# Sparse attention heads of a two-block layer: masks and gates prepared once, fewer VectorE operations per head, exponentials in one piece

## The reference, cut to what matters

```python
s_c = einsum(qb, kc) * scale + head_bias(dist_c)
p_c = masked_softmax(s_c, dist_c >= 0)          # exp masked again, sum kept above 1e-30
p_s = masked_softmax(s_s, dist_s >= 0)
p_w = masked_softmax(s_w, mask_w)
o = g0 * (p_c @ vc) + g1 * (p_s @ vs) + g2 * (p_w @ vw)   # gates g: one per position, head and branch
```

## Time and profile before

| | us |
|---|---|
| median of 3 runs (4032.55 to 4039.31) | 4033.61 |
| the profiled execution | 4030.8 |
| its span, first instruction to last | 4028.9 |
| busy in the span: PE / DVE / ACT / POOL | 3857.7 / 1769.7 / 600.3 / 1241.4 |

### The profile page before, as it was taken

How to read it: one execution, slowest core, us unless ns; L and a number is a source line. 1 busy time by engine, 2 the same in 40 slices (tenths; PEclk the granted TensorE clock), 3 DMA queues, 4 the chain that set the end, 5 groups by cost and what they waited for, 6 DMA issues and landing times.

```text
span 4028.9 us, 65270 instructions
## 1 busy us (share of the span) xinstructions
PE 3857.7 (96%) x28244; PEld 3561.4 (88%) x28244; DVE 1769.7 (44%) x3203; ACT 600.3 (15%) x1315; POOL 1241.4 (31%) x783
## 2 busy tenths in 40 slices
PE   8999999999999999999999999997798899999997
PEld 7888888888788998999999998776597899999997
DVE  1344425540313513111144455723422688887544
ACT  0333311111111011000000000222302211111001
POOL 0000000003222774777740000001150477775000
PEclk9999999999999999999999999998899999999999
DMA  6566654456654443444444554354142344444442
GB/s 239 195 225 225 220 207 170 160 191 215 194 179 159 155 168 110 170 170 171 170 158 160 172 206 170 140 128 158 45 160 97 115 168 168 168 168 163 167 158 79
DMA packets 109118, 668.81 MB, mean 166 GB/s; under 512 B 23056, under 2 KB 27472, under 8 KB 78496
## 3 DMA queue, kind: packets, MB, share of 16 engines
q1 hardware_dynamic: 64208, 549.01, 37.6%
q0 software_dynamic: 21088, 69.73, 5.8%
q10 hardware_dynamic: 23536, 45.92, 3.2%
HBM read 611.34 MB, written 53.25 MB: 165 GB/s over the span
## 4 chain that ended last, share of the span: by engine, by line
PE 89%; DVE 4%; issue 3%; ACT 2%; POOL 1%; POOLq 1%; DVEq 1%; ACTq 1%; DMA 0%
PE product_bank L550 46%; PE product_bank L598 31%; PE product_bank L392 3%; PE mixer_bank L742 1%; PE mixer_bank L758 1%; POOL arena L519 1%; POOLq L521 1%; POOLq L518 0%; POOL arena L522 0%; ACT xT L859 0%; PE mixer_bank L1271 0%; PE mixer_bank L1285 0%; PE mixer_bank L1122 0%; ACTq L2276 0%; DVE arena L1357 0%
## 5 line engine op out<-in xcount | busy, mean ns | idle before, releaser
L598 PE MATMUL product_bank<-hT,weight_ring 128*128 128x256 f32 x3648 | 812.4, 381 | 0.0
L598 PEld LDWEIGHTS product_bank<-hT,weight_ring 128*128 128x128 f32 x3648 | 689.5, 190 | 103.2 <-issue 10.2
L550 PE MATMUL product_bank<-hT,weight_ring 128*128 128x128 f32 x3680 | 457.6, 277 | 14.1 <-DVEq L1628 5.8
L550 PEld LDWEIGHTS product_bank<-hT,weight_ring 128*128 128x128 f32 x3680 | 435.8, 193 | 16.7 <-issue 6.8
L550 PE MATMUL product_bank<-arena,weight_ring 128*128 128x128 f32 x3200 | 398.5, 275 | 0.0
L550 PEld LDWEIGHTS product_bank<-arena,weight_ring 128*128 128x128 f32 x3200 | 378.5, 192 | 0.6
L517 POOL TENSOR_TENSOR arena<-weight_ring 128x1024 f32<-128x1024 f32 x89 | 212.8, 2391 | 479.5 <-PE product_bank L550 307.7
L574 DVE TENSOR_TENSOR arena<-product_bank,arena 128x128 f32<-128x128 f32 x127 | 36.9, 290 | 730.9 <-PE product_bank L550 730.9
L2601 DVE SCALAR_TENSOR_TENSOR arena<-arena 128x256 f32<-128x256 f32 x176 | 322.4, 1870 | 14.2 <-ACT arena L2566 10.9
L520 POOL TENSOR_TENSOR weight_ring<-weight_ring 128x1024 f32<-128x1024 f32 x111 | 272.1, 2452 | 0.0
L550 PE MATMUL product_bank<-hT,arena 128*128 128x128 f32 x2048 | 250.9, 277 | 0.2 <-DVE hT L506 0.2
(11 more groups left out here) (495 smaller groups left out, 5353.3 us busy)
## 6 DMA issues: line engine op xcount, KB each, us to landing
weight_ring<-in_weights SPq DMA_DIRECT2D x213, 2048.0 KB, 8.0
weight_ring<-in_weights SPq DMA_DIRECT2D x128, 512.0 KB, 5.6
weight_ring<-in_weights SPq DMA_DIRECT2D x64, 384.0 KB, 5.8
units<-out_stage ACTq DMA_DIRECT2D x87, 256.0 KB, 7.8
rwkv_keep<-arena ACTq DMA_DIRECT2D x16, 1282.0 KB, 6.1
arena<-rwkv_keep POOLq DMA_DIRECT2D x8, 1280.0 KB, 7.3
arena<-units POOLq DMA_DIRECT2D x36, 256.0 KB, 3.4
arena<-units POOLq DMA_DIRECT2D x48, 128.0 KB, 6.0
```

The lines of the kernel that those rows point to most:

```text
L550: mm = pe.matmul(bank[:, at * P:at * P + P], lhs[:, j, :], rhs[:, j, :], start=g == 0 and n in (0, 3) and j == 0, stop=g == n_groups - 1 a ...
L598: mm = pe.matmul(psg[b][:, half * T:half * T + T], lhs, rhs, start=k == 0, stop=k == 15)
```

## The change

In the sparse heads only, nothing on PE, POOL or SP is edited. Before the loop DVE scales the compressed bias by 8, adds the mask to it for all heads at once, and lays out the gates of all heads in one array, with the rows that see no compressed block set to zero. In the loop the compressed scores are one operation (L2325 goes), the four maxima are two over pairs, the two negations are one, the mask on the exponentials (L2340) and the floor (L2344) go, the two gate products are one, and the two scalings of the compressed part are one. On ACT all exponentials of head h+1 stand together, ahead of the wait for head h's output and of its copy.

```diff
-        n_H, n_kc, n_vc, n_pos = carve(120, 64, 256, 2, at=at + 2 * sum(NSA_BUFS))
+        n_H, n_kc, n_vc, n_pos, n_gate = carve(120, 64, 256, 2, 96, at=at + 2 * sum(NSA_BUFS))
...
+        ngate = n_gate.rearrange("p (h w q) -> p h w q", w=3, q=2)
...
-            def exponentials(h, w):
+            def exponentials(h):
                 n_s, n_pt, n_cs, n_ct, n_st = nsa_bufs[h % 2]
                 act.wait_ge(sem("attn_max"), NSA_SOFT_AT + h + 1)
-                for qb, (a, z) in enumerate([(256, 384), (0, 256)]):
-                    n = 2 * w + qb
-                    s = n_s[:, 384 * w + a:384 * w + z]
-                    act.activation(s, s, ACT.Exp, scale=HSCALE, bias=n_st[:, 8 + n:9 + n],
-                                   accum_out=n_st[:, 16 + n:17 + n])
-                if w == 0:
-                    return
+                for w in range(2):
+                    for qb, (a, z) in enumerate([(256, 384), (0, 256)]):
+                        n = 2 * w + qb
+                        s = n_s[:, 384 * w + a:384 * w + z]
+                        act.activation(s, s, ACT.Exp, scale=HSCALE, bias=n_st[:, 8 + n:9 + n],
+                                       accum_out=n_st[:, 16 + n:17 + n])
                 for qb in range(2):
                     s = n_cs[:, 16 * qb:16 * qb + 15]
-                    act.activation(s, s, ACT.Exp, bias=n_st[:, 12 + qb:13 + qb])
+                    act.activation(s, s, ACT.Exp, scale=HSCALE, bias=n_st[:, 12 + qb:13 + qb])
                 act.drain().then_inc(sem("attn_exp"), 1)
 
-            exponentials(0, 0)
-            exponentials(0, 1)
+            exponentials(0)
             for h in range(NH):
...
                 act.drain().then_inc(sem("attn_pt"), 1)
                 if h + 1 < NH:
-                    exponentials(h + 1, 0)
+                    exponentials(h + 1)
                 act.wait_ge(sem("attn_out"), NSA_AT_HEAD + h + 1)
                 act.activation(hT[r, 8 + b, :], bank[0][r, 0:256], ACT.Copy).then_inc(sem("attn_head_done"), 1)
-                if h + 1 < NH:
-                    exponentials(h + 1, 1)
                 if h in (5, 11):
                     store_unit(act, *LATE[3 + h // 6])
...
-            dve.tensor_copy(nBC, pm[1][:, 0:480].rearrange("p (q n h) -> p q h n", q=2, h=NH))
+            dve.tensor_scalar(nBC, pm[1][:, 0:480].rearrange("p (q n h) -> p q h n", q=2, h=NH), 1 / HSCALE, None, ALU.mult)
             dve.drain().then_inc(sem("bias_rows_ready"), 1)
             dve.wait_ge(sem("bias_rows_stored"), 16)
             dve.wait_ge(sem("nsa_gates"), 1)
...
+            dve.tensor_tensor(nBC, nBC, cadd.unsqueeze(2).to_broadcast([P, 2, NH, NCMP]), ALU.add)
+            by_head = ng.rearrange("p q (h w) -> p h w q", w=3)
+            dve.tensor_copy(ngate[:, :, 0:2, :], by_head[:, :, 1:3, :])
+            dve.tensor_tensor(ngate[:, :, 2, :], by_head[:, :, 0, :], cmul[:, :, 0].unsqueeze(1).to_broadcast([P, NH, 2]),
+                              ALU.mult)
+            dve.drain()
             for h in range(NH):
...
-                dve.scalar_tensor_tensor(cs, bank[0][:, 384:416].rearrange("p (q n) -> p q n", q=2)[:, :, 0:15], HSCALE,
-                                         nBC[:, :, h, :], ALU.mult, ALU.add)
-                dve.drain()
-                dve.tensor_tensor(cs, cs, cadd, ALU.add)
+                dve.tensor_tensor(cs, bank[0][:, 384:416].rearrange("p (q n) -> p q n", q=2)[:, :, 0:NCMP], nBC[:, :, h, :],
+                                  ALU.add)
                 dve.wait_ge(sem(f"nsa_bias{h % 2}"), 32 * (h // 2 + 1))
...
-                for w in range(2):
-                    dve.reduce_max(n_st[:, 2 * w:2 * w + 1], n_s[:, 384 * w + 256:384 * w + 384], AX.X)
-                    dve.reduce_max(n_st[:, 2 * w + 1:2 * w + 2], n_s[:, 384 * w:384 * w + 256], AX.X)
-                dve.drain()
+                dve.reduce_max(n_st[:, 0:4:2], both[:, :, 256:384], AX.X)
+                dve.reduce_max(n_st[:, 1:4:2], both[:, :, 0:256], AX.X)
                 dve.reduce_max(n_st[:, 4:6], cs, AX.X)
                 dve.drain()
-                dve.tensor_scalar(n_st[:, 8:12], n_st[:, 0:4], -HSCALE, None, ALU.mult)
-                dve.tensor_scalar(n_st[:, 12:14], n_st[:, 4:6], -1.0, None, ALU.mult).then_inc(sem("attn_max"), 1)
+                dve.tensor_scalar(n_st[:, 8:14], n_st[:, 0:6], -HSCALE, None, ALU.mult).then_inc(sem("attn_max"), 1)
                 dve.wait_ge(sem("attn_exp"), NSA_SOFT_AT + h + 1)
-                dve.tensor_tensor(cs, cs, cmul, ALU.mult)
-                dve.drain()
                 dve.reduce_sum(n_st[:, 20:22], cs, AX.X)
                 dve.drain()
-                dve.tensor_scalar(n_st[:, 16:22], n_st[:, 16:22], 1e-30, None, ALU.max)
-                dve.drain()
                 dve.reciprocal(n_st[:, 16:22], n_st[:, 16:22])
                 dve.drain()
-
-                f = n_st[:, 24:30].rearrange("p (w q) -> p q w", w=3)
-                s = n_st[:, 16:22].rearrange("p (w q) -> p q w", w=3)
-                dve.tensor_tensor(f[:, :, 0:2], s[:, :, 0:2], ng[:, :, 3 * h + 1:3 * h + 3], ALU.mult)
-                dve.tensor_tensor(f[:, :, 2:3], s[:, :, 2:3], ng[:, :, 3 * h:3 * h + 1], ALU.mult)
+                dve.tensor_tensor(n_st[:, 24:30], n_st[:, 16:22], n_gate[:, 6 * h:6 * h + 6], ALU.mult)
                 dve.drain()
                 for w in range(2):
...
-                for qb in range(2):
-                    v = n_cs[:, 16 * qb:16 * qb + 15]
-                    last = dve.tensor_scalar(v, v, n_st[:, 28 + qb:29 + qb], None, ALU.mult)
-                last.then_inc(sem("attn_probs"), 1)
+                dve.tensor_tensor(cs, cs, n_st[:, 28:30].unsqueeze(2).to_broadcast([P, 2, NCMP]), ALU.mult)\
+                    .then_inc(sem("attn_probs"), 1)
```

More of the change, by code:

```diff
@@ L2319, in nsa_dve @@
                 bank = nsa_banks(h)
-                cs = n_cs.rearrange("p (q n) -> p q n", q=2)[:, :, 0:15]
+                cs = n_cs.rearrange("p (q n) -> p q n", q=2)[:, :, 0:NCMP]
+                both = n_s.rearrange("p (w n) -> p w n", w=2)
                 dve.wait_ge(sem("attn_scores"), NSA_AT_HEAD + h + 1)
-                dve.scalar_tensor_tensor(cs, bank[0][:, 384:416].rearrange("p (q n) -> p q n", q=2)[:, :, 0:15], HSCALE,
-                                         nBC[:, :, h, :], ALU.mult, ALU.add)
-                dve.drain()
-                dve.tensor_tensor(cs, cs, cadd, ALU.add)
+                dve.tensor_tensor(cs, bank[0][:, 384:416].rearrange("p (q n) -> p q n", q=2)[:, :, 0:NCMP], nBC[:, :, h, :],
+                                  ALU.add)
                 dve.wait_ge(sem(f"nsa_bias{h % 2}"), 32 * (h // 2 + 1))
                 for w in range(2):
-                    dve.tensor_tensor(n_s[:, 384 * w:384 * w + 384], bank[w][:, 0:384], nbias[:, h % 2, :], ALU.add)\
+                    dve.tensor_tensor(both[:, w, :], bank[w][:, 0:384], nbias[:, h % 2, :], ALU.add)\
                         .then_inc(sem("nsa_biased"), 1)
                 dve.drain()
-                for w in range(2):
-                    dve.reduce_max(n_st[:, 2 * w:2 * w + 1], n_s[:, 384 * w + 256:384 * w + 384], AX.X)
-                    dve.reduce_max(n_st[:, 2 * w + 1:2 * w + 2], n_s[:, 384 * w:384 * w + 256], AX.X)
-                dve.drain()
+                dve.reduce_max(n_st[:, 0:4:2], both[:, :, 256:384], AX.X)
+                dve.reduce_max(n_st[:, 1:4:2], both[:, :, 0:256], AX.X)
                 dve.reduce_max(n_st[:, 4:6], cs, AX.X)
                 dve.drain()
-                dve.tensor_scalar(n_st[:, 8:12], n_st[:, 0:4], -HSCALE, None, ALU.mult)
-                dve.tensor_scalar(n_st[:, 12:14], n_st[:, 4:6], -1.0, None, ALU.mult).then_inc(sem("attn_max"), 1)
+                dve.tensor_scalar(n_st[:, 8:14], n_st[:, 0:6], -HSCALE, None, ALU.mult).then_inc(sem("attn_max"), 1)
                 dve.wait_ge(sem("attn_exp"), NSA_SOFT_AT + h + 1)
-                dve.tensor_tensor(cs, cs, cmul, ALU.mult)
-                dve.drain()
                 dve.reduce_sum(n_st[:, 20:22], cs, AX.X)
-                dve.drain()
-                dve.tensor_scalar(n_st[:, 16:22], n_st[:, 16:22], 1e-30, None, ALU.max)
                 dve.drain()
```

## The result

The changed kernel takes 4004.69 us in the median of 4 runs (4000.66 to 4007.26), the kernel before 4033.08 beside it: a ratio of 0.9924, 95% interval 0.9908 to 0.9939, so 28 us less. 4004.0 was predicted. The profiled execution of the changed kernel took 4000.66 us, the lowest of its four, with a span of 3998.9, 30.0 less than the span of before.

The account below looks back on a forecast made before the run. No engine is full; a loop of waits between PE, ACT and DVE bounds the sparse heads. 10.0 + 17.0 + 3.0 + 0.2 = 30 off the profiled 4030.8 gives 4001, plus 2.8 for the median: 4004 us, range 3995 to 4015.

Parts of the forecast that it names:

- Even steps: Eight even steps of the sparse heads: from 90.2 to 73.2 us, PE binding, mostly at 2.4 GHz; 17.0 us gained.
- The rival with the low clock: PE stays at 1.2 GHz at the start of even steps, 1.6 us more in each of four: 4011; chance 0.14.
- Plain odd steps: Steps 3, 5, 9, 11, 13 of the sparse heads: 9.4 becomes 7.4 us each; 10.0 us gained.
- PE binds: In the new odd step PE's side, 7.3 to 7.4 us, narrowly outlasts DVE's 7.1.
- The POOL steps: Steps 1 and 7, where POOL sums weights: 12.5 to 15.0 and 10.7 to 13.2 us; 3.0 us gained, from 0.5 to 5.6.
- the middle I took: Steps 1 and 7: gain of 3.0 us, taken between scalings before L522 and scalings waiting for its end.
- the strict reading: Steps 1 and 7: each scaling can be caught by a POOL instruction; the total ends 2.5 us later, at 4006.
- Head 0: Before and in head 0: 1.1 us of operations added, front and back give back 1.3; 0.2 us gained.
- Removed operations only: Rival: ACT and PE hinder each other, leaving 1.25 us in each of 16 steps, 20 in all: 4014; chance 0.09.
- Given back in `out2`: Rival: out2's weights arrive no earlier than now, so PE waits there: 4033; chance 0.03.
- Slower: Rival: grouped maxima with strided results run far below one element per cycle: 4045; chance 0.04.
- X = 6.5: X is the time from scores to maxima, 2.65 expected; at 6.5 each of 7 step pairs loses 1.6 us: 4045.

Follow-up runs that it names:

- e2_dve_only: The changed kernel with the ACT order of before (exponentials in two pieces, the second behind head h's output): 4015.25 us.
- e1_act_only: The kernel before with the ACT edit alone (exponentials in one piece): 4014.99 us.
- e3_back_undone: The changed kernel with the mask on the compressed exponentials and the floor 1e-30 put back into each head: 4008.14 us.
- e4_front_undone: The changed kernel with four maxima and two negations per head again, ahead of the exponentials: 4008.71 us.
- e7_memory_behind: The changed kernel with one memory product whole in step 0 and the other two behind the last head: 4058.69 us.
- the halves: The kernel before with the ACT edit alone, and the changed kernel with the ACT order of before: 18.7 and 18.4 us under the kernel before.
- e6_sums_spread: The changed kernel with each of POOL's two sums of weights cut into three parts, one ahead of the loads of each odd head 5 to 15: 3986.82 us.
- e8_sums_gaps: The changed kernel with POOL's eight sum instructions sent one at a time, each after VectorE gives a head's maxima: 3996.03 us.

## Why the prediction was right, point by point

- **Even steps, 17.0 forecast.** They gave 17.1: the eight took 90.1 before and take 73.0. PE became the bound, and at 2.4 GHz: 8.55, where 8.7 was taken. The closeness of the sum is partly luck: step 0 took 11.04 where 10.4 was taken, 0.6 too little, and the four plain steps and step 14 (6.94 for 7.2) together 0.9 too much. That the clock stays up after a wait under 1 us, a choice in the prediction, held here and, for waits of 1.42, in `e2_dve_only`. The rival with the low clock, at 4011, did not come in this kernel; it did in single steps of `e1_act_only`, `e3_back_undone` and `e4_front_undone`. The prediction says that every even step of the kernel before starts at 1.2 GHz; steps 4 and 6 start at 2.4 (first transpose 0.33 us) and the clock falls just behind, for a grant of 0.85 and 0.84 over the step, so the reading holds for their lengths.
- **Plain odd steps, 10.0 forecast.** 10.35. The order of events was right to 0.1: maxima at 2.67 (2.65 forecast), exponentials 2.31, copy at 5.06 (5.0). The back is 1.87 where 2.04 was taken, which costs nothing here, as it has slack. "PE binds" was right in that the scores release the turn, but loosely put: PE's own work is 6.75 of 7.40. What binds is the chain through the copy, as `e4_front_undone` and `e7_memory_behind` show.
- **The POOL steps, 3.0 forecast, from 0.5 to 5.6.** 2.1, between the middle I took and the 0.5 of the strict reading. The path was that of the strict reading, which ends behind L522, but with 0.3 from L522's end to the turn where 1.3 was taken: step 1 is 1.3, 12.5 of the sum and 0.3, 14.1 in all. The Trainium skill (SBUF — State Buffer, SBUF: two separate sides) has the engine that starts first hold the shared ports for the whole instruction and lets reductions pass; the rows agree: the maximum L2336 takes its 0.68 beside L517, the negation L2339 ends as L517 ends, the gates L2345 get in 0.05 before L519 starts, and three of the four scalings stand behind one POOL instruction each.
- **Head 0, 0.2 forecast.** From VectorE's start to the turn it was 8.22 us (2749.45 to 2757.67) and is 7.78, 0.4 less: the added work takes 0.95 (2749.96 to 2750.91) where 1.1 was taken. But that execution reached the stage 0.5 later (row below), so turn 0 lies at 2757.74.

The added work of head 0, in VectorE's timeline after (L2318 and L2319 follow it, 0.19 and 0.20), against the earlier trace rows:

```profile
2749.96 0.66 DVE L2316 TENSOR_TENSOR arena<-arena,consts 128x480 f32<-128x480 f32 x1 [54.31 <-ACT arena L2262]
```

- **Removed operations only, 4014.** Excluded: the halves are not additive, and 0.53 us put back cost 0.1 per odd step and nothing in even ones.
- **Given back in `out2`, 4033.** The rest of the span is 1099.5 where it was 1100.1.
- **Slower, 4045.** The maxima over pairs take 0.42 and 0.68 with strided results; to be slower than before, by the prediction's estimate the front would have had to last 3 us longer than it does.

The sum was 30; 29.4 came in this stage (179.4 to 150.0), 0.6 in the rest of the span. The parts miss by +0.1, +0.35, -0.9 and +0.2, so that the total is closer than its POOL term. Against the runs' median the gain is 28.4: the profiled execution lay 4.0 under the median after and 2.3 before. Small slips in the prediction change none of this: the upper bound of the POOL steps is 5.5 by its own figures (28.7 less 23.2), its own range 4001 to 4008 and not 4000 to 4009, the loss at X = 6.5 is 1.5 per pair and not 1.6.

## What to carry to other kernels

Write the loop between engines as a sum of stretches and put each engine's own work beside it as a floor: the gain of an edit is its share up to that floor, and two edits that reach the same floor do not add. After such a change look for what is late next; here it was another engine's work in one piece, whose cost depended on where it lay, and cutting it up gave 18 us more for a few lines. Order the copies of one engine so that no wait for a slow neighbour stands ahead of work that is already due.

## What the runs showed of the hardware

- TensorE's clock fell to 1.2 GHz in single steps after short waits of PE: 0.65 us (`e3_back_undone`, step 6), 0.65 and 0.39 (the same, step 12), 1.00 (`e4_front_undone`, steps 6 and 12), 1.27 and 0.29 (`e1_act_only`, step 4). It did not fall after the same 1.27 and 0.29 four more times in `e1_act_only`, after 0.47 and 1.42 (`e2_dve_only`, five times), after 1.68 (`e6_sums_spread`, step 5) nor after 0.65 in the changed kernel (two profiles). In the kernel before it fell each time after 0.47 and 2.17 (steps 4, 6, 10, 12 and 14). Each fall in a variant cost 1.6 to 1.7 us. What decides it after the shorter waits stays open.
- With 5.1 us of PE work per step the clock stayed at 1.2 GHz over three steps of 11.1, although the same steps take 7.34 at 2.4 GHz (`e7_memory_behind`). PE was busy 9.35 of the 11.1 us.
- VectorE's scalings of 128x128 and 128x256, 1.01 us for four by themselves, took 2.24, 2.44 and 2.43 us one by one where each began up to 0.2 us behind a TENSOR_TENSOR of POOL of 2.35 to 2.40, and ended 0.1 to 0.2 us behind its end; the one between two took 0.27. Maxima beside the same work took their 0.42 and 0.68 (step 1 of the changed kernel).
- A POOL instruction behind a drain and a wait stood 1.73 to 1.97 us for nothing that the profile shows, in seven cases of eight, and 1.7 to 2.4 us passed from VectorE's maxima to its start (`e8_sums_gaps`).
